# A diffusion block with a mixture of experts: expert weights read as four adjacent rows per partition

## What is computed

```python
# six modulation vectors of 2048 for the latent tokens, two used for the context
mods = split(silu(c) @ w_mod + b_mod, 6)          # w_mod 2048 x 12288
n    = rmsnorm(x, attn_norm) * (1 + scale) + shift
p    = n @ w_in                                    # attention ranks and gated convolution
h    = x + gate * (concat(attention, conv) @ w_out)
m    = rmsnorm(h, ffn_norm) * (1 + scale_f) + shift_f
idx, w = route(m @ w_router + bias)                # 4 of 32 experts for each token
y    = sum_e w_e * (silu(m @ w_exp_gate[e]) * (m @ w_exp_up[e])) @ w_exp_down[e]
y   += (silu(m @ w_sh_gate) * (m @ w_sh_up)) @ w_sh_down
out  = rmsnorm(h + gate_f * y, final_norm)
```

## Time and profile before

| | us |
|---|---|
| median of 3 runs | 1299.01 (1298.03 to 1299.72) |
| the profiled execution | 1298.86 |
| its span, first to last instruction | 1297.1 |
| outside the span | 1.8 |
| TensorE busy | 1187.3 (92%) |
| VectorE busy | 606.7 (47%) |
| ScalarE busy | 262.0 (20%) |
| packets of SP's loads | 276,304, 379.1 MB |
| mean granted TensorE clock | 0.978 |

### The profile page before, as it was taken

One profiled execution on the slowest core, in us unless ns is written; L12 is line 12 of the kernel. 1 busy time (PEld: TensorE's weight loads), 2 busy tenths in 40 slices (PEclk: granted clock), 3 DMA queues, 4 the chain that ended last, 5 costly groups with the idle time before them and its releaser, 6 DMA issues.

```text
span 1297.1 us, 17313 instructions
## 1 busy us (share of the span) xinstructions
PE 1187.3 (92%) x6261; PEld 644.4 (50%) x6262; DVE 606.7 (47%) x1211; ACT 262.0 (20%) x550; POOL 8.7 (1%) x13
## 2 busy tenths in 40 slices
PE   2779999999999999989998999999999999999973
PEld 0424588888744544448663444434444444444420
DVE  0200396558167668552622444444444444444417
ACT  4211200000024510012001222222222222222203
POOL 0000000000000000000000000000000000000001
PEclk9989999999999999999998999999999999999986
DMA  9999989998375389972377999983999999999961
GB/s 339 345 349 350 301 294 368 347 329 288 107 256 197 127 296 387 345 276 92 109 244 249 361 361 361 361 286 99 361 361 361 360 358 358 358 359 361 361 217 65
DMA packets 276339, 379.60 MB, mean 293 GB/s; under 512 B 12675, under 2 KB 182865, under 8 KB 274641
## 3 DMA queue, kind: packets, MB, share of 16 engines
q1 hardware_dynamic: 276304, 379.14, 85.9%
HBM read 377.01 MB, written 2.10 MB: 292 GB/s over the span
## 4 chain that ended last, share of the span: by engine, by line
PE 79%; DVE 7%; issue 4%; ACT 4%; DMA 3%; SPq 1%; POOL 0%; POOLq 0%; DVEq 0%; ACTq 0%
PE ps L491 77%; DMA ring<-in_w_mod 3%; ACT nreg L939 3%; DVE nreg L1642 3%; DVE part L1634 2%; PE ps L861 1%; SPq L317 1%; SPq L309 0%; PE ps L784 0%; DVE tiny L1399 0%; PE ps L561 0%; DVE nreg L1646 0%; PE ps L736 0%; PE ps L878 0%; DVE xres L1649 0%
## 5 line engine op out<-in xcount | busy, mean ns | idle before, releaser
L491 PE MATMUL ps<-nreg,ring 128*128 128x256 f32 (+1 forms) x1280 | 299.1, 394 | 10.3 <-ACT nreg L939 5.9
L491 PEld LDWEIGHTS ps<-nreg,ring 128*128 128x128 f32 x1280 | 242.6, 191 | 63.6 <-issue 21.9
L491 PE MATMUL ps<-ring,nreg 128*64 128x512 f32 x1088 | 240.9, 601 | 0.0
L1252 DVE SCALAR_TENSOR_TENSOR part<-ring,csT,part 128x512 f32<-128x512 f32 x240 | 180.4, 752 | 9.2
L491 PEld LDWEIGHTS ps<-ring,nreg 128*64 128x64 f32 x1088 | 77.4, 139 | 151.8 <-issue 151.8
L491 PE MATMUL ps<-ring,conv 128*64 128x512 f32 x544 | 128.0, 602 | 0.5 <-ACT conv L939 0.5
L491 PE MATMUL ps<-nreg,conv 128*128 128x512 bf16 x374 | 96.4, 384 | 16.9 <-DVE nreg L1642 13.5
L491 PE MATMUL ps<-ring 128*128 128x512 f32 x256 | 110.8, 592 | 0.0
L491 PE MATMUL ps<-pick,qnT 128*128 128x128 bf16 x544 | 94.9, 220 | 0.6 <-issue 0.6
L491 PE MATMUL ps<-pick,hb 128*128 128x128 bf16 x544 | 94.5, 219 | 0.0
L491 PE MATMUL ps<-pick,kq 128*128 128x128 bf16 x544 | 94.5, 219 | 0.0
(11 more groups left out here) (201 smaller groups left out, 881.5 us busy)
## 6 DMA issues: line engine op xcount, KB each, us to landing
ring<-in_w_mod SPq DMA_DIRECT2D x88, 1024.0 KB, 9.5
ring<-in_w_exp_gate SPq DMA_DIRECT2D x128, 512.0 KB, 8.6
ring<-in_w_exp_up SPq DMA_DIRECT2D x128, 512.0 KB, 8.7
ring<-in_w_exp_down SPq DMA_DIRECT2D x128, 512.0 KB, 9.6
ring<-in_w_in SPq DMA_DIRECT2D x15, 2048.0 KB, 11.9
ring<-in_w_out SPq DMA_DIRECT2D x8, 2048.0 KB, 10.7
ring<-in_w_mod SPq DMA_DIRECT2D x4, 2048.0 KB, 19.9
ring<-in_w_sh_up SPq DMA_DIRECT2D x2, 2048.0 KB, 10.2
```

What stands on the lines that cost most here:

```text
L491: return nc.tensor.matmul(o, l, r, start=start, stop=stop)
L1252: ins = V.scalar_tensor_tensor(out=acc, in0=w, scalar=scale, in1=acc, op0=ALU.mult, op1=ALU.add)
```

## The change

A quarter q of the features (512 rows) is dealt out differently: partition p gets the rows 512q + 4p + j for j = 0 to 3, which are adjacent in memory. So chunk 4q + j, partition p now holds feature 512q + 4p + j. For an expert's gate or up one partition's part of a quarter is then one run of 4 KB. Down loads bring 1024 columns of two rows (4 KB pieces), four loads of 1 MB a pair in place of eight of 512 KB, with two semaphores in place of four. The router's weights come as 512-byte pieces instead of 128. The shared expert's gate and up keep pieces of 1 KB, but each 2 MB load is issued as four of 512 KB.

Everything that is multiplied with these rows has to follow the new order:

- `xh` is written in it: VectorE and ScalarE read `xres` with a step of four floats, and write runs of 128.
- The shift and scale columns: the last of 16 steps of `accumulate` for groups 8 to 15 writes to `sorted_part` (in the tile `qnT`) with a step of 128 floats, and `mod_sum_cols` reads that.
- Their bias and `ffn_norm` are loaded once more in the new order (`bT2`, `fnT`), by three loads of 512 pieces of 16 bytes. They stand in SP's program behind the convolution loop. VectorE waits for them (`cols_in`) before it adds the bias. The loads at the start stay.

```diff
-        wg = w_exp_gate[0].rearrange("e (c p) n -> p e c n", p=P)
+        wg = w_exp_gate[0].rearrange("e (q p j) n -> p e q (j n)", q=4, j=4)
-        sg = w_sh_gate[0].rearrange("(c p) n -> p c n", p=P)
+        sg = w_sh_gate[0].rearrange("(q p j) n -> p q j n", q=4, j=4)
...
+        def by_row(v, n):
+            return v.rearrange("p (j c) -> p j c", c=n)
+        def by_col(v):
+            return v.rearrange("p (c j) -> p j c", j=4)
...
+            for at, src in ((bT2[:, 0:KC], b_mod[0, 3 * D:4 * D]), (bT2[:, KC:2 * KC], b_mod[0, 4 * D:5 * D]),
+                            (fnT[:, :], ffn_norm[0])):
+                sp.dma_start(at.rearrange("p (q j) -> p q j", q=4), src.rearrange("(q p j) -> p q j", q=4, j=4))\
+                  .then_inc(cols_in, 16)
...
+            def load_shared(s, src, half):
+                for q in range(4):
+                    sp.dma_start(k_of(s, KC)[:, 4 * q:4 * q + 4, :], src[:, q, :, FF * half:FF * half + FF])\
+                      .then_inc(w_full[s], 16)
...
-                sp.dma_start(down[u][:, :, 512 * n:512 * n + 512],
-                             wd[:, bass.ds(2 * i + u, 1), :, 512 * n:512 * n + 512]
+                sp.dma_start(down[u][:, :, 1024 * n:1024 * n + 1024],
+                             wd[:, bass.ds(2 * i + u, 1), :, 1024 * n:1024 * n + 1024]
...
                         for a in range(3):
-                            if n < 3 and h == a == 0 and last:
-                                ins.then_inc(down_used[n + 1], 1)
+                            if n in (0, 2) and h == a == 0 and last:
+                                ins.then_inc(down_used[n // 2], 1)
...
-                    pe.wait_ge(down_in[n], 32 * i + 32)
+                    if n % 2 == 0:
+                        pe.wait_ge(down_in[n // 2], 32 * i + 32)
...
-                            if n == 1 and k == u == 0 and last:
-                                ins.then_inc(down_used[0], 1)
...
-                nc.scalar.activation(xh[:, 1, 512 * n:512 * n + 512], xres[:, 1, 512 * n:512 * n + 512], ACT.Identity,
+                nc.scalar.activation(by_row(xh[:, 1, 512 * n:512 * n + 512], 128), by_col(xres[:, 1, 512 * n:512 * n + 512]),
...
+                            if by_feature and q == k == 3:
+                                out_, w_, acc_ = (by_row(sorted_part[:, b, :], 128).rearrange("p j c -> p c j"),
+                                                  w.rearrange("p (c j) -> p c j", j=4), acc.rearrange("p (c j) -> p c j", j=4))
...
+            ve.wait_ge(cols_in, 48)
...
-                V.tensor_scalar(xh[:, 0, 512 * n:512 * n + 512], xres[:, 0, 512 * n:512 * n + 512], stat[:, 10:11], None,
+                V.tensor_scalar(by_row(xh[:, 0, 512 * n:512 * n + 512], 128), by_col(xres[:, 0, 512 * n:512 * n + 512]),
```

More of the change, by code:

```diff
@@ L104, in block_kernel @@
         bT = sb("bT", [P, 96])
+        bT2 = sb("bT2", [P, 2 * KC])
+        fnT = sb("fnT", [P, KC])
         amul = sb("amul", [P, KC, 2])
@@ L158, in block_kernel @@
         yacc = nreg[:, 4096:8192].rearrange("p (t d) -> p t d", t=2)
+        sorted_part = qnT[:, 0:4, :].rearrange("p h t -> p (h t)").rearrange("p (b n) -> p b n", b=2)
         shT = krT[:, :].rearrange("p (k t) -> p k t", k=2)
@@ L224, in block_kernel @@
         gu_used = [sem(f"gu_used{q}") for q in range(4)]
-        down_in = [sem(f"down_in{n}") for n in range(4)]
-        down_used = [sem(f"down_used{n}") for n in range(4)]
+        down_in = [sem(f"down_in{n}") for n in range(2)]
+        down_used = [sem(f"down_used{n}") for n in range(2)]
         pick_ready, pickw_ready, gx_full, gx_act, gx_dve, pickT_full, pickT_out = (
@@ L233, in block_kernel @@
         y_high, y_rest, y_mid, weight_ready = sem("y_high"), sem("y_rest"), sem("y_mid"), sem("weight_ready")
+        cols_in = sem("cols_in")
         mean_sq, root, mean_wide, root_wide = sem("mean_sq"), sem("root"), sem("mean_wide"), sem("root_wide")
@@ L276, in block_kernel @@
         SH_SLOT = (0, 1, 2, 0, 4, 5)
-        SH_USE = (11, 10, 11, 12, 1, 2)
+        SH_USE = (14, 13, 14, 18, 1, 2)
         block = stack.enter_context(nc.Block())
@@ L360, in _ @@
             sp.dma_start(k_of(2, 2), wkv).then_inc(w_full[2], 16)
-            sp.dma_start(wr[:, :, :], w_router[0].rearrange("(c p) n -> p c n", p=P)).then_inc(router_in, 16)
+            sp.dma_start(wr[:, :, :].rearrange("p (q j) n -> p q (j n)", q=4),
+                         w_router[0].rearrange("(q p j) n -> p q (j n)", q=4, j=4)).then_inc(router_in, 16)
             sp.dma_start(rb[:, :], router_bias.to_broadcast([P, NE])).then_inc(router_in, 16)
@@ L398, in _ @@
             sp.wait_ge(wo_full, 3)
[L399 removed]
+            def load_shared(s, src, half):
+                for q in range(4):
+                    sp.dma_start(k_of(s, KC)[:, 4 * q:4 * q + 4, :], src[:, q, :, FF * half:FF * half + FF])\
+                      .then_inc(w_full[s], 16)
+            load_shared(1, su, 0)
             sp.wait_ge(wo_half, 4)
[L401 removed]
+            load_shared(2, sg, 1)
             sp.wait_ge(acc_done, 16 * 16)
@@ L404, in _ @@
             sp.wait_ge(wo_full, 4)
-            sp.dma_start(k_of(0, KC), sg[:, :, 0:FF]).then_inc(w_full[0], 16)
+            load_shared(0, sg, 0)
             sp.dma_start(k_of(5, 2), sd[:, 2:4, :]).then_inc(w_full[5], 16)
             sp.wait_ge(sh_gate, 2)
-            sp.dma_start(k_of(0, KC), su[:, :, FF:2 * FF]).then_inc(w_full[0], 16)
+            load_shared(0, su, 1)
             def load_quarter(i, q):
@@ L431, in _ @@
             sp.wait_ge(sh_down, 8)
-            for n in range(4):
+            for n in range(2):
                 load_down(0, n, 0)
@@ L517, in mod_sum_cols @@
                 for j in range(4):
-                    ins = mm(ps[:, 5, j:j + 1], part[:, b, 128 * j:128 * j + 128], ones[:, 0:1], True, True)
+                    ins = mm(ps[:, 5, j:j + 1], sorted_part[:, b, 128 * j:128 * j + 128], ones[:, 0:1], True, True)
                 ins.then_inc(mod_cols, 1)
@@ L1237, in cols_out, with accumulate @@
                     .then_inc(modT_done, 1)
-            def accumulate(n, b, slots_=mslot, quarters=range(4)):
+            def accumulate(n, b, slots_=mslot, quarters=range(4), by_feature=False):
                 acc = part[:, b, :]
@@ L1251, in accumulate @@
                             ve.wait_ge(acc_done, 16 * (n - 8) + (4 * q + k))
-                            ins = V.scalar_tensor_tensor(out=acc, in0=w, scalar=scale, in1=acc, op0=ALU.mult,
+                            out_, w_, acc_ = acc, w, acc
+                            if by_feature and q == k == 3:
+                                out_, w_, acc_ = (by_row(sorted_part[:, b, :], 128).rearrange("p j c -> p c j"),
+                                                  w.rearrange("p (c j) -> p c j", j=4), acc.rearrange("p (c j) -> p c j", j=4))
+                            ins = V.scalar_tensor_tensor(out=out_, in0=w_, scalar=scale, in1=acc_, op0=ALU.mult,
                                                          op1=ALU.add)
@@ L1335, in tap @@
                     return vecT[:, bass.ds(V_CW + 8 * j + m + 2 * i, 1)]
-                accumulate(2 * i + 8, 0)
-                accumulate(2 * i + 9, 1)
+                accumulate(2 * i + 8, 0, by_feature=True)
+                accumulate(2 * i + 9, 1, by_feature=True)
                 for m in range(2):
```

19 lines of the change are left out of this document (8 added, 11 removed).

## The result

| | before | after |
|---|---|---|
| median (range), 20 runs each | 1298.7 (1297.0 to 1300.42) | 1300.85 (1297.26 to 1303.16) |
| ratio, 95% interval | | 1.0017, 1.001 to 1.0024 |
| the profiled execution | 1298.86 | 1301.01 |
| its span | 1297.1 | 1299.2 |
| mean granted TensorE clock | 0.978 | 0.974 |

A forecast was written before the change was run, and what follows sets the result against it. The prediction took the expert stage to be bound by TensorE, with the loads close behind. Span 1297.1 + 1.0 for the `xh` read + 1.8 outside = 1299.9, set at 1300.0 us after a 0.15 median offset; range 1294.5 to 1304.

The forecast's parts named there:

- What bounds the kernel: Expert stage: bound by TensorE at 34.28 us a pass, loads close behind at 34.94, lead left 7 us or more.
- slower pieces: Expert loads, rival: 4 KB pieces move below 355 GB/s and passes follow the loads; +24 us at 340 GB/s; chance 0.05.
- 4 KB pieces: Expert gate, up and down loads: 401 GB/s, 31.4 us a pair instead of 34.9, none on the path; value 0.
- Down in two waits: Expert down loads: buffers freed and waited for in two halves instead of four quarters; value 0.
- Small loads: SP's queue before `w_q_b`: three loads of 16-byte pieces could hold SP up to 5.7 us; value 0.
- Last step of `accumulate`: Column sums, groups 8 to 15: strided write costs 0 to 0.8 us each, eight times, covered by 17 us; value 0.
- `xh` with a step: Second norm, the one edit on the path: 0 to +2 us, middle +1.0 us taken.
- The faster rival: Two TensorE "issue" stalls at entry and last pass: emptier queue cuts 2 us from each, 1292.5 to 1296; chance 0.15.
- The norm beyond a doubling: Second norm, slower rival: stepped xh read costs more than double, from 2.6 us on, 1303 to 1304; chance 0.14.

The follow-up runs named there:

- extra_before: The kernel before with 1.05 MB more to load in each turn of the expert loop: 1313.39 us, ratio 1.012.
- gate_up_alone: The kernel before with only the experts' gate and up read in 4 KB pieces, output not the reference's: 1298.87 us, ratio 0.9999.
- down_alone: The kernel before with only the changed down loads (1024 columns, four a pair, two semaphores): 1298.19 us, ratio 0.9996.
- plain_xh: The changed kernel with only the stepped read of xh undone, output not the reference's: 1298.77 us, ratio 0.9995.
- held_after_split: The changed kernel with down loads held back at both stalls and one of ScalarE's four xh pieces given to VectorE: 1292.27 us, ratio 0.9956.

## Why the prediction was right, point by point

- **What bounds the kernel.** Right. TensorE's passes are 34.3 us in every kernel but extra_before, with loads of 34.9 us a pair and with less. That the product period and not the load rate bounds the stage rested on two rows seven passes apart. Extra_before shows the point at which it would turn, and the lead did run out there. One reading was wrong: the lead doesn't shrink by 10 us over fifteen passes. The slices 286 and 99 in the earlier trace rows are the second pass over one pair, at which it is filled up, and it shrinks by 9 x 0.66 = 6 us behind it. So the loads had more room than the prediction gave them, and its bound of 355 GB/s for slower pieces was too strict. Nor does have the 2.6 us that it names as the shortest landing of a down load; that is 3.9. The forecast rests on neither.
- **4 KB pieces.** The rate was 410 GB/s where 401 was taken from the 3 KB row. The value was 0, and gate_up_alone measures 0.9999.
- **Down in two waits.** The value was 0, and down_alone measures 0.9996. Not foreseen: the entry stall grows by 0.5 us with the 4 KB pieces, too little to be seen in the total.
- **Small loads.** The three loads take 0.93 + 0.52 = 1.5 us of SP, below the bound of 5.7, and the load behind the router's is issued in 0.50 us where 7.54 stood. Neither moves the end. VectorE's wait on `cols_in` is not among the waits. SP's queue after:

```profile
306.20 0.93 SPq L367 DMA_DIRECT2D bT<-in_b_mod  x2
307.17 0.52 SPq L367 DMA_DIRECT2D fnT<-in_ffn_norm  x1
307.73 12.54 SPq L371 DMA_DIRECT2D ring<-in_w_q_b  x2
...
335.54 0.50 SPq L377 DMA_DIRECT2D rb<-in_router_bias  x1
```

- **Last step of `accumulate`.** It was bounded at 0 to 0.8 us more each. The group of after by line and shape (busy us, mean ns) has 1117 ns, where the other 232 steps have 752: +0.37 us eight times, hidden as said.

```profile
L1274 DVE SCALAR_TENSOR_TENSOR qnT<-ring,csT,part 128x512 f32<-128x512 f32 x8 | 8.9, 1117 | 0.3
```

- **`xh` with a step: the term that was mis-sized.** It was the right edit, on the path, and the middle value of +1.0 us is what the norm stage shows as a mean (+1.1). But the change cost 2.2, and plain_xh takes all of it back. So the total of 1300.85 lies near 1300.0 with a term of half the size of the loss. The groups of after:

```profile
L1111 ACT ACTIVATE ring<-xres,stat 128x512 f32<-128x512 f32 x4 | 4.6, 1220 | 1.2 <-POOL stat L492 1.2
...
L1492 DVE TENSOR_SCALAR ring<-xres,stat 128x512 f32<-128x512 f32 x4 | 2.5, 681 | 0.8 <-POOL stat L492 0.8
```

Four pieces in a row are 4.59 us on ScalarE where the earlier trace rows has 2.56, that is 1.15 us a piece against 0.64 (x1.8). The profile's mean of one piece is 1220 ns against 710, a little longer, since successive pieces overlap. VectorE's mean goes from 481 to 681 ns. I expected VectorE to lose the most and ScalarE to have room; it was ScalarE. The sum missed what a late ScalarE does to TensorE: it stops in the middle of the transposes for 0.62 us, and in some executions then stays at 1.2 GHz through the rest of them, which costs 1.7 us more. The timeline of after:

```profile
579.40 3.65 PE L803 MATMUL ps<-cst,ring 128*128 128x128 f32 x16 [5.33 <-DVE ring L1492]
...
583.67 1.97 PE L803 MATMUL ps<-cst,ring 128*128 128x128 f32 x16 [0.62 <-ACT nreg L1118]
```

That this stop is what keeps the clock low wasn't shown: after has the stop and the full clock behind it. Only, none of the seven plain profiles has such a stage, nor has held_after_split, which has the step without the stop. The rest, half of the 2.2 us or more, is a path that the prediction doesn't have: TensorE's clock behind the two stalls, +0.9 us in the first pass and +0.5 in the last as a mean over the profiles. The prediction priced the `xh` edit in the norm only and let nothing follow from it. That the total came within 0.9 us is in part luck: 2.2 us stand where 1.0 was set, and before's median was 0.3 us lower in the 20 runs than in the three. Why the clock comes back later stays open.

The Trainium skill (Advanced Engine Details and Errata, section Memory Cachelines) says that a read which goes to another line each time is penalised, and gives no size; the doubling was the prediction's own reading of it. The trace agrees with the penalty: x1.8 on ScalarE and x1.5 on VectorE (0.62 us against 0.42 from start to start). The sum of +2 that the prediction worked out from a doubling is nearer to the measured 2.2 than its +1.0, but for another reason, since only 1.1 of that is in the norm.

- **The faster rival.** Its mechanism is real and its condition wasn't met. I gave it 2 us a stall, and it is 3 at the entry and 2.2 to 2.6 at the last. But the change leaves loads moving beside both stalls (238 GB/s at the entry and 206 at the last). It lengthened the first by 0.46 us and shortened the last by 0.32. It had to be held against what the change does (smaller gaps, not fewer loads), which is what the prediction's "against" said.
- **The norm beyond a doubling**, 2.6 us or more. Two of six profiles come near it or reach it, at +2.2 and +2.6 us, by the clock and not by the read itself, which stayed under a doubling.
- **Slower pieces.** Fell at 410 GB/s.

## What to carry to other kernels

Before making loads lighter, measure the period of the loads and that of the compute at the same two places many turns apart: here 34.94 against 34.28 with a lead that lasted to the last pass meant that nothing could be gained. Look on the way for a place where the loads wait and the lead is filled up again. Then ask which stage pays for the new layout: here the gain was hidden in every pass, while the cost began at one place where TensorE waits for two engines. And look for "issue" stalls at the entry to a loop and behind it: holding bulk loads back for those few microseconds gave 5 to 6 us, which 115,000 packets fewer did not.

## What the runs showed of the hardware

- **TensorE's "issue" stalls at the entry to its expert loop and behind it depend on the load traffic.** At the entry 6.8 to 7.4 us with 238 (after) and 261 GB/s (before) beside it, 3.6 to 3.9 us with next to none; at the last pass 6.2 to 6.7 with 375 beside it in before, and 3.9 to 4.4 with the loads held. The length doesn't simply follow the rate: after's last stall is 6.22 us with 206 GB/s beside it. The window of held_after_split at the last:

```profile
1232.80:1236.70 3.90, 0.00 (x0) 0.00 (x0) 1.54 (x4) 0.00 (x0) 0.00 (x0) 0.98 0.02 4
```

The page of the kernels lists instructions as a queue among those of the DMA engines (packets, MB, share of the span), here for after:

```profile
q8 instruction: 22, 0.36, 0.1%
```

The Trainium skill (Runtime: NRT & Kernel Launch, section Instruction fetch mechanics) states that a taken branch out of the fetched window has to fetch by DMA before execution goes on. The two stalls stand where TensorE enters and leaves its loop, and grow with the loads beside them, which agrees; which packets belong to them no run here shows.

- **The entry stall depends on the pieces of that traffic too:** 4 KB pieces of down lengthen the entry stall by 0.5 us against 2 KB pieces, in five profiles against five.
- **Rates by piece on this core:** 348, 388 and 401 GB/s for 1, 2 and 3 KB, and 410 for 4 KB.
- **A read with a step of four floats** costs ScalarE x1.8 and VectorE's tensor_scalar x1.5; a write with a step of 512 bytes costs VectorE's scalar_tensor_tensor x1.5.
- **The last 16 transposes of one kernel's norm stage ran at either clock** in different executions: 10.76 and 12.43 us for the stage, of the same code.
- **TensorE's clock falls to 1.2 GHz in or at the end of each of the two stalls and comes back 2.4 to 5.3 us into the products.** From there on that costs half of the time spent at it: 1.7 us of the first pass in before, 2.7 in after.
